# Later rounding of the weights of items 19 to 31, and one rest moved behind the scaling of q

## The reference

```
z = rms_norm(h) @ w_in                                  # 1024 x 3584
u, v, g_a, q, k, vv, g_b = split(z)                     # 512 columns each
y_a = gelu(u) * (tril(W_s) @ layer_norm(gelu(v)) + b) * silu(g_a)
y_b = softmax(mask(q k^T / 8)) vv * silu(g_b)           # 8 heads of 64
h = h + concat(y_a, y_b) @ w_out
```

## Time and profile before

| what | value |
|---|---|
| time, median of 3 runs | 276.67 us (276.58 to 276.71) |
| profiled execution | 275.13 us, span 273.3 us |
| TensorE busy | 96% of the span |
| weight load busy | 85% |
| VectorE busy | 66% |
| ScalarE busy | 58% |
| mean DMA rate | 163 GB/s |

### The profile page before, as it was taken

How to read it: one execution, slowest core, us unless ns; L and a number is a source line. 1 busy time by engine, 2 the same in 40 slices (tenths; PEclk the granted TensorE clock), 3 DMA queues, 4 the chain that set the end, 5 groups by cost and what they waited for, 6 DMA issues and landing times.

```text
span 273.3 us, 4264 instructions
## 1 busy us (share of the span) xinstructions
PE 261.1 (96%) x1598; PEld 231.8 (85%) x1598; DVE 179.3 (66%) x327; ACT 159.1 (58%) x301; POOL 24.2 (9%) x52
## 2 busy tenths in 40 slices
PE   7999999959999999999999999999999999999990
PEld 6789997848888888887888999999998888988880
DVE  2975998967694788557758709393945858532643
ACT  4875857787466453637366646658666675640132
POOL 3016310000100000001100000200003001000021
PEclk9999999997999999999999999999999999999997
DMA  7999739482248144444447950735143441100004
GB/s 234 396 393 372 258 115 352 156 299 61 101 134 284 45 153 156 153 153 156 156 153 248 342 179 21 287 111 199 29 163 118 153 157 31 49 0 0 2 1 153
DMA packets 22452, 44.59 MB, mean 163 GB/s; under 512 B 1056, under 2 KB 1312, under 8 KB 22432
## 3 DMA queue, kind: packets, MB, share of 16 engines
q1 hardware_dynamic: 21712, 43.00, 45.7%
q10 hardware_dynamic: 576, 0.79, 0.8%
q0 software_dynamic: 144, 0.52, 0.6%
HBM read 43.26 MB, written 1.05 MB: 162 GB/s over the span
## 4 chain that ended last, share of the span: by engine, by line
PE 69%; DVE 13%; DMA 8%; ACT 5%; issue 3%; ACTq 0%; POOLq 0%; POOL 0%; DVEq 0%
PE products L1000 14%; PE products L1002 14%; PE products L1001 14%; DVE w_lo L740 6%; DMA w_raw<-in_ab_w_in 6%; PE products L963 5%; PE products L961 5%; PE products L959 5%; PE turned L911 3%; DVE k_low L786 3%; DMA y<-in_x_turned 2%; PE attended L1043 2%; PE attended L1044 2%; PE attended L1042 2%; PE scores L1020 1%
## 5 line engine op out<-in xcount | busy, mean ns | idle before, releaser
L740 DVE TENSOR_TENSOR w_lo<-w_raw,w_hi 128x1024 fp32r<-128x1024 f32 x74 | 89.0, 1227 | 9.8 <-ACT w_hi L602 9.1
L602 ACT CAST w_hi<-w_raw 128x1024 fp32r<-128x1024 f32 x74 | 75.9, 1047 | 31.3 <-PE products L1002 15.1
L959 PE MATMUL products<-hnT_hi,w_hi 128*128 128x256 f32 x192 | 54.7, 285 | 0.0
L963 PE MATMUL products<-hnT_hi,w_lo 128*128 128x256 f32 x192 | 54.3, 283 | 0.0
L961 PE MATMUL products<-hnT_lo,w_hi 128*128 128x256 f32 x192 | 54.3, 283 | 0.0
L1000 PE MATMUL products<-w_hi,hnT_hi 128*128 128x512 f32 x128 | 51.9, 405 | 0.1
L1002 PE MATMUL products<-w_lo,hnT_hi 128*128 128x512 f32 x128 | 50.5, 394 | 0.0
L1001 PE MATMUL products<-w_hi,hnT_lo 128*128 128x512 f32 x128 | 50.5, 394 | 0.0
L959 PEld LDWEIGHTS products<-hnT_hi,w_hi 128*128 128x128 f32 x192 | 36.7, 191 | 0.5 <-DVE w_lo L740 0.5
L961 PEld LDWEIGHTS products<-hnT_lo,w_hi 128*128 128x128 f32 x192 | 36.8, 192 | 0.0
L963 PEld LDWEIGHTS products<-hnT_hi,w_lo 128*128 128x128 f32 x192 | 36.7, 191 | 0.0
(11 more groups left out here) (144 smaller groups left out, 361.3 us busy)
## 6 DMA issues: line engine op xcount, KB each, us to landing
w_raw<-in_c_w_in SPq DMA_DIRECT2D x16, 1024.0 KB, 5.5
w_raw<-in_ab_w_in SPq DMA_DIRECT2D x12, 1024.0 KB, 5.7
w_raw<-in_ab_w_out SPq DMA_DIRECT2D x4, 1024.0 KB, 5.0
w_raw<-in_c_w_out SPq DMA_DIRECT2D x4, 1024.0 KB, 5.0
w_raw<-in_ab_w_in SPq DMA_DIRECT2D x4, 256.0 KB, 4.9
w_raw<-in_ab_w_in SPq DMA_DIRECT2D x2, 512.0 KB, 7.7
h<-in_x SPq DMA_DIRECT2D x2, 512.0 KB, 11.1
out<-hn SPq DMA_DIRECT2D x4, 256.0 KB, 2.2
```

What stands on the lines that cost most here:

```text
L602: nc.scalar.copy(w_hi[:, n % SPLIT_SLOTS, :, :], w_raw[:, half % RAW_SLOTS, part, :]).then_inc(hi_ready, 1)
L740: nc.vector.tensor_tensor(w_lo[:, n % SPLIT_SLOTS, :, :], w_raw[:, half % RAW_SLOTS, part, :], w_hi[:, n % SPLIT_SLOTS, :, :].bitcast(fp32 ...
L959: nc.tensor.matmul(to, wh, hi[:, chunk, :], start=begins and c % 2 == 0, stop=False, skip_group_check=True)
L963: last = nc.tensor.matmul(to, wl, hi[:, chunk, :], start=False, stop=ends, skip_group_check=True)
```

## The change

The table `LAST_ROUND` gets entries for items 14 to 23, so that the rounds ahead of these items run only about four items ahead of their use. Before, rounds 21 to 24 all stood ahead of item 16; now round 20 stands there, round 21 ahead of item 17, and so on; from item 24 on both orders are the same. The rests follow their rounds. Of the rest that stands ahead of item 11 (rest 15) it changes the place: `LAGS[11]` is 1, and when q's group ends that rest is written between `scale_heads` and `evacuate`. The number of instructions of each kind stays.

```diff
-LAST_ROUND = {2: 6, 3: 7, 4: 9, 5: 9, 6: 9, 7: 9, 8: 11, 9: 13, 10: 14, 11: 15, 12: 15, 13: 17, 14: 19, 15: 20}
-LAGS = {4: 0, 5: 0, 6: 0, 7: 0, 8: 1, 9: 1, 10: 1, 11: 0, 12: 4, 13: 4, 14: 1, 15: 1}
+LAST_ROUND = {2: 6, 3: 7, 4: 9, 5: 9, 6: 9, 7: 9, 8: 11, 9: 13, 10: 14, 11: 15, 12: 15, 13: 17, 14: 18, 15: 19, 16: 20,
+              17: 21, 18: 22, 19: 23, 20: 25, 21: 26, 22: 28, 23: 30}
+LAGS = {4: 0, 5: 0, 6: 0, 7: 0, 8: 1, 9: 1, 10: 1, 11: 1, 12: 4, 13: 4, 14: 1, 15: 1}
...
             if g in (1, 2):
                 out.append(("scale_heads", g))
                 if g == 1:
                     out += [("round", split), ("rest", split)]
                     split += 1
+                else:
+                    out.append(("rest", rounded.pop(0)))
             out.append(("evacuate", g))
```

## The result

The changed kernel takes 269.86 us, median of 4 runs (269.50 to 270.23), against 276.69 us before (median of 4 runs, 276.58 to 277.02). The ratio is 0.9751, 95% interval 0.9734 to 0.9768. I had forecast 271.4 with a range of 270.8 to 272.9: the direction was right, the size 5.30 where 6.83 came, and the range missed the time by 0.9 us.

The account below looks back on a forecast made before the run. TensorE, busy 261.1 of 273.3 us, was taken as the bound, with only idle and slow time to win. Gains 0.65 + 4.75 = 5.40, less 0.10, gave 5.30 off the median 276.67: 271.4 us, range 270.8 to 272.9.

Parts of the forecast that it names:

- Rest 15 behind the scaling: Ahead of scores 0: q's low parts on DVE come earlier, so scores start earlier; gain 0.65 us, between 0 and 0.74.
- Rounds 21 to 24 out of the way: Ahead of values 0: gelu_inner 3 and the `probsT` copy come 3.78 us earlier; wait and slow stretch vanish, gain 4.75 us.
- The 0.1 for the tight places: Allowance of 0.1 us taken off the 5.40 us gain for all places where PE's margins become small.
- The price of the slow clock: Behind the gap ahead of values 0, to item 18: PE at 1.2 GHz costs 1.68 us beyond the 3.07 wait.
- a new wait: Rival, chance 0.18: at one of five tight places PE waits 0.5 to 1.5 us, giving 271.9 to 272.9 us.
- the place that was named with its own clock: Values 3: transpose 7's copy stands behind round 28, which waits for half 14's load; forecast to hold with 0.29 us spare.
- The slower case: Chance 0.04: half 14 lands so late that values 3 stand still and the clock falls; 279.3 us at a 12 us landing.
- the case of no effect: Chance 0.04: values 0 still wait as long, for a reason the trace hides; 276.1 to 277 us.
- the second rival: Chance 0.07: the slow clock behind the gap isn't in the timed runs, so only waits are won; 273.05 us.

Follow-up runs that it names:

- the filled gap: The kernel before with 12 unread products of ones ahead of values 0, the wait for the copy left in place: 273.09 us, ratio 0.9900.
- the second profile: Profiled execution of the kernel before, run again unchanged: 277.89 us, among 12 runs of 273.02 to 277.89 us.

## Why the prediction was right or wrong

**Rest 15 behind the scaling**: right mechanism, over-sized. The term was 0.65; scores 0 moved by 0.67 from one profile to the other (45.42 to 44.50, less 0.25 for the earlier start), but the runs give 0.2 to 0.5, since the wait there is 0.2 in three of the five profiles with the old order, those that start slowly, and 0.5 or 0.6 in the other two. I had read it from one of these two.

**Rounds 21 to 24 out of the way**: right in every place. gelu_inner 3 came 0.01 from the forecast, once the 0.25 is taken off; the wait is gone; values 3 start at 83.26 where 83.51 - 0.25 = 83.26 was forecast. The wait of 3.07 is confirmed as paid in full by the filled gap (273.09) against the changed kernel: 273.09 - 269.86 = 3.23, for the 3.07 and what the moved rest gives. The two numbers are of different sets, so this is good to a few tenths. The 0.1 for the tight places wasn't needed in the profiled execution.

**The price of the slow clock is the term that was mis-sized**: 1.68 in my sum, 3.0 us in the usual run of before, by the filled gap and by the second profile. The step that failed is in the sentence "I expect the same difference and subtract from the median". The 1.54 us between the profiled execution and the timed runs wasn't an offset of the measurement. Most of it was a dearer slow stretch in the very thing that the change removes (276.2 against 274.9 in the median of the two groups, 1.3 us). The three timed runs, 0.13 us apart and all longer than the profiled one, were the hint. With 3.01 in place of 1.68 the sum would have been 6.63 and the time 270.0. Had all of the 1.54 been added, it would have been 6.84 and 269.8, but that near hit would have been luck in part: the rest's 0.65 was too large by 0.15 to 0.45. What the experiments price is 3.07 + 3.0 + 0.2 to 0.5, that is 6.3 to 6.6 of the 6.83; the last 0.3 to 0.5 is about what the runs of before beside the result lay above their group (276.69 against 276.21), and is open.

The Trainium skill, TensorE: Matmul & The Clock Gate, Part 1, which I had weighed, says that the chip's look at the engine's activity is free-running, and that how many slow matmuls a kernel starts with varies from run to run; that a gap in mid-kernel is charged differently, too, was my inference. The 67 runs of before at three levels of mean clock, 273.3, 274.9 and 276.2 us, agree with it. I let it speak for the cheap side, as a rival with 273.05, and gave the dear side only the 0.3 us by which the range reaches below my forecast's own. It should have been weighed by the timed runs, which were longer than the profiled one.

**The rivals**: a new wait exists, in the place that was named with its own clock: 0.8 us in one of the changed kernel's two profiles, 270.76 us long, where its other nine runs took 269.50 to 270.23. The Trainium skill, DMA: Bandwidth & Descriptors, section Bandwidth, has 6.15 us for 1 MB, measured with loads that GpSimd issued (here SyncE does). That is nearer to this execution's 6.55 us than the 4.9 to 6.0 of the stretch that I had taken as bounds. The slower case and the case of no effect didn't come. The cheap slow clock of the second rival exists, in 4 of 67 runs of before, but not as the usual case.

## What to carry to other kernels

When a profiled execution and the timed runs of the same kernel differ by more than the timed runs among themselves, first find which part of the program differs, and take the price of that part from the timed runs: here a dozen repeated runs with the mean granted clock of each told it at once. A gap on TensorE can be worth more than its own length, because the clock behind it differs from run to run (waits of 1.29 us and more drew it down here, though not in every run); filling the gap with unneeded products bought 3.0 us here without touching the wait. And in an order shared by several engines a step that waits for a transfer doesn't belong ahead of a short copy for which TensorE waits.

## What the runs showed of the hardware

Behind the same wait of 2.9 to 3.0 us the clock can stay as it is, or be at 1.2 GHz for a shorter or a longer stretch, at a price of 1.68 us in one profile, 3.01 and 3.30 in two others: 273.3, 274.9 and 276.2 us. With a wait of 1.7 us 3 of 6 runs had a slow stretch by their mean clock, with 2.6 us 6 of 10, with 2.9 us 63 of 67, with 0.7 us none of 4; yet one of 1.29 us at another place drew the clock down in one run, and one of 1.54 us in another kernel did not. Nothing here shows what decides between the three. The first products of the program can run at 1.2 GHz for longer or shorter, which the clock column doesn't show and the durations do (two matmuls of 512 columns in 1.05 or in 0.62 us); it moved scores 0 by 1.4 and 2.1 us in two executions. And a load of 1 MB issued at the same place in the program took 5.0 us in one execution and 6.55 in another.
